# A two-layer hybrid decoder on one core: the first head's gates made alone, every fourth early sum on VectorE, and identity products ahead of two TensorE stages

## The reference, cut to what matters

```python
for l in range(2):                                  # x is (1, 512, 1024) float32
    h = rmsnorm(x, norm1_g[l]); z = h @ w_in[l]     # 3080 columns
    mixed = [norm(attention(8 heads of 64)), norm(chunked_gmlp), norm(short_conv)]
    x = x + mixed @ w_out[l]
    h2 = rmsnorm(x, norm2_g[l])
    q = h2 @ w_query[l]                             # 8 heads, two halves of 128
    s1, s2 = q_half . sub_keys                      # 128 keys each
    v1, i1 = top_k(s1, 16); v2, i2 = top_k(s2, 16)
    sc, ci = top_k(v1[:, None] + v2[None, :], 16)   # 16 of 256 pairs
    expert = i1[ci // 16] * 128 + i2[ci % 16]       # one of 16384 rows
    gate = softmax(sc)
    x = x + sum_k gelu(expert_u[expert_k] . h2) * gate_k * expert_v[expert_k]
out = rmsnorm(x, final_g)
```

## The time and the profile before

| | |
|---|---|
| median of 3 executions | 2962.34 us (2959.41 to 2963.81) |
| the profiled execution | 2957.96 us, its span 2956.2 us |
| mean granted TensorE clock | 0.83 of full |
| busy: PE, DVE, ACT, POOL | 2379.9, 1981.1, 1259.0, 1236.9 us |
| DMA | 1192.27 MB, mean 403 GB/s; the gathers 1073.81 MB |

### The profile page before, as it was taken

One profiled execution on the slowest core, in us unless ns is written; L12 is line 12 of the kernel. 1 busy time (PEld: TensorE's weight loads), 2 busy tenths in 40 slices (PEclk: granted clock), 3 DMA queues, 4 the chain that ended last, 5 costly groups with the idle time before them and its releaser, 6 DMA issues.

```text
span 2956.2 us, 38032 instructions
## 1 busy us (share of the span) xinstructions
PE 2379.9 (81%) x12592; PEld 940.0 (32%) x12592; DVE 1981.1 (67%) x4731; ACT 1259.0 (43%) x3735; POOL 1236.9 (42%) x1063
## 2 busy tenths in 40 slices
PE   8799988888967887787976898888896667767665
PEld 6633445344612332242421233323351111111110
DVE  2666566887468757877448766887647777777544
ACT  2242543863344337734334434753333333333333
POOL 0232343444344434444334444444434544555452
PEclk9899988998967998897976998888897665566666
DMA  9699999999999999999999999999999999999997
GB/s 360 231 379 357 381 390 416 421 420 419 414 417 418 412 416 414 412 408 420 417 414 411 415 410 420 410 407 419 420 419 421 410 421 421 421 406 421 421 421 299
DMA packets 202349, 1192.27 MB, mean 403 GB/s; under 512 B 25384, under 2 KB 38184, under 8 KB 68520
## 3 DMA queue, kind: packets, MB, share of 16 engines
q0 software_dynamic: 147456, 1073.81, 88.2%
q1 hardware_dynamic: 54696, 116.03, 10.4%
HBM read 1187.67 MB, written 2.10 MB: 402 GB/s over the span
## 4 chain that ended last, share of the span: by engine, by line
DMA 44%; PE 32%; DVE 10%; ACT 7%; issue 6%; POOL 2%; POOLq 0%; DVEq 0%; ACTq 0%
DMA arena<-in_uv,eidx 41%; PE acc L1793 12%; PE bank L1485 9%; DVE arena L1471 5%; PE bank L1727 4%; PE bank L1567 3%; DMA unit<-in_w_in 2%; POOL arena L803 2%; ACT L1039 1%; ACT diag L1048 1%; ACT wts L1042 1%; PE heads L1485 1%; DMA unit<-in_w_query 1%; PE bank L1690 1%; ACT L936 1%
## 5 line engine op out<-in xcount | busy, mean ns | idle before, releaser
L803 POOL DMA_INDIRECT arena<-in_uv,eidx x1024 | 1202.2, 1174 | 1531.6 <-PE acc L1793 1305.4
L1793 PE MATMUL acc<-arena,diag 64*64 64x512 f32 x8192 | 1404.4, 772 | 519.1 <-ACT diag L1048 486.5
L1471 DVE CUSTOM_DVE_ANT_0 arena<-arena,h 128x1024 f32<-128x1024 f32 x1024 | 1254.2, 1226 | 771.6 <-DMA arena<-in_uv,eidx 765.0
L1039 ACT ACTIVATE gelu<-dots 128x1 f32<-128x1 f32 x1024 | 206.1, 201 | 1346.4 <-DVE dots L1471 1345.0
L1793 PEld LDWEIGHTS acc<-arena,diag 64*64 64x64 f32 x8192 | 256.6, 155 | 1357.3 <-ACT diag L1048 1170.5
L1048 ACT ACTIVATE diag<-identc,wts 128x64 f32<-128x64 f32 x1024 | 356.1, 348 | 33.6
L1042 ACT ACTIVATE wts<-gelu,gate 128x1 f32<-128x1 f32 x1024 | 301.4, 294 | 33.2
L1727 PE MATMUL bank<-h,unit 128*128 128x256 f32 (+1 forms) x1024 | 231.1, 372 | 6.9 <-DMA unit<-in_w_query 6.9
L1727 PEld LDWEIGHTS bank<-h,unit 128*128 128x128 f32 x1024 | 171.3, 195 | 116.6 <-issue 92.5
L1485 PE MATMUL bank<-unit,h 128*128 128x512 f32 (+1 forms) x336 | 139.9, 545 | 0.0
L1567 PE MATMUL bank<-h,unit 128*128 128x256 f32 (+2 forms) x480 | 125.6, 405 | 0.0
(11 more groups left out here) (207 smaller groups left out, 1735.5 us busy)
## 6 DMA issues: line engine op xcount, KB each, us to landing
unit<-in_w_in SPq DMA_DIRECT2D x36, 1024.0 KB, 20.8
unit<-in_w_query SPq DMA_DIRECT2D x35, 1024.0 KB, 12.0
arena<-in_uv,eidx POOLq DMA_INDIRECT x1024, 17.3
unit<-in_w_out SPq DMA_DIRECT2D x16, 1024.0 KB, 9.6
arena<-in_w_in SPq DMA_DIRECT2D x8, 1024.0 KB, 11.7
arena<-in_w_query SPq DMA_DIRECT2D x5, 1024.0 KB, 19.6
arena<-in_w_out SPq DMA_DIRECT2D x4, 1024.0 KB, 14.3
x<-in_x SPq DMA_DIRECT2D x4, 512.0 KB, 10.1
```

Source lines behind the costliest of these rows:

```text
L803: nc.gpsimd.indirect_dma_start(arena[:, n % NBUF, :], None, uv, bass.IndirectOffsetOnAxis(ap=eidx[:, seq % 2, j:j + 1], axis=0)).then_inc( ...
L1039: nc.scalar.activation(gelu[:, group], dots[:, group], ACT.Gelu_apprx_tanh).then_inc(s_ge, GROUP)
L1471: V.tensor_tensor_reduce(out=uu, in0=uu, in1=h_nat[seq % 3], scale=1.0, scalar=0.0, op0=ALU.mult, op1=ALU.add, accum_out=dots[:, n % BODY: ...
L1793: ins = nc.tensor.matmul(acc[rows][cols * HALF:(cols + 1) * HALF, :], diag[own, n % NBUF, :], arena[own, n % NBUF, D + f * 512:D + (f + 1) ...
```

## The change

Four parts, all in the first 128 slots or before them.

1. **Gates of the first head alone.** Ahead of slot 0 VectorE makes head 0's numbers and, at once, head 0's gates; head 1 becomes chunk 0 of the routing plan, 19 parts from slot 0 on, two a slot, its exponential at slot 5. Chunk 1 moves from slot 3, two a slot, to slot 10, three a slot. The exponential of chunk 0 is split in two, each over one head.
2. **Sums by VectorE.** Slots 11, 15, 19, ... 111 (26 of them) get no `diag` and no matmuls. VectorE adds weight times `expert_v` to `x` with one `scalar_tensor_tensor` of 128x1024, issued behind the dot two slots later. A semaphore of its own, `s_vsum`, frees these buffers.
3. **Identity products.** 12 float32 products of the 128x128 identity at TensorE's start, and 14 between the output product and `T2` of the first pass. Nothing reads their result.
4. ScalarE squares two constants into a scratch tile before it waits for `x`.

```diff
+WARM_START, WARM_NORM = 12, 14
+VEC_LAG = 2
+SECOND_HEAD, SECOND_CHUNK = (0, 2), (10, 3)
+    def on_vector(n):
+        return n % 4 == 3 and 8 <= n < SLOTS - 16
     def route_at(r):
+        if r <= 1:
+            return SECOND_HEAD if r == 0 else SECOND_CHUNK
-        return (3, 2) if r == 1 else (first_slot(p) + 27 * (c - 1) + ..., 1)
# GpSimd, ScalarE: buffer n - NBUF
-                    pool.wait_ge(s_used, n - NBUF + 1)
+                    wait_summed(pool, n - NBUF)      # s_vsum if on_vector, else s_used
# ScalarE
             act.wait_ge(s_setup, 10)
+            nc.scalar.activation(junk16[:, 0:2], ones[:], ACT.Square)
...
+                if on_vector(n):
+                    continue                          # no diag
# VectorE, first pass
                 if p == 0:
-                    for _ in routing(l, 0, 0):
-                        pass
+                    first_head(l, 0)
+                    ask_exp(0, 1)
+                    take_gates(0, 0, 0, 1, 0)
+            def add_weighted(n):
+                t = tile_of[n // SLOTS]
+                dve.wait_ge(s_wt, n + 1)
+                if sums_by_vector(n):
+                    dve.wait_ge(s_vsum, sums_by_vector(n))
+                V.scalar_tensor_tensor(out=x[:, t, :], in0=arena[:, n % NBUF, D:2 * D], scalar=wts[:, n % BODY:n % BODY + 1],
+                                       in1=x[:, t, :], op0=ALU.mult, op1=ALU.add).then_inc(s_vsum, 1)
...                                                   # in the slot loop, behind the dot of slot n
+                if n >= VEC_LAG and on_vector(n - VEC_LAG):
+                    add_weighted(n - VEC_LAG)
# TensorE
+                if p == 0:
+                    wait_freed(pe, p, "CS")
+                    keep_clock(WARM_NORM)
                 yield from idle(NORM_STEPS)           # then T2
+            def keep_clock(n):
+                for _ in range(n):
+                    mm(acc[1][:, 0:P], ident[:], ident[:], True, True)
             pe.wait_ge(s_setup, 10)
+            keep_clock(WARM_START)
...                                                   # in the slot loop
+                if on_vector(n):
+                    continue                          # no matmuls
+                pe.wait_ge(s_dg, sums_by_tensor(n + 1))
```

More of the change, by code:

```diff
@@ L335, in due, with sums_by_tensor, sums_by_vector @@
         return steps_done(n) if n >= 0 else steps_ahead()
+    def on_vector(n):
+        return n % 4 == 3 and 8 <= n < SLOTS - 16
+    def sums_by_tensor(n):
+        return sum(not on_vector(m) for m in range(n))
+    def sums_by_vector(n):
+        return sum(on_vector(m) for m in range(n))
     def route_at(r):
         seq = r // CHUNKS
+        if r <= 1:
+            return SECOND_HEAD if r == 0 else SECOND_CHUNK
         if seq in first_seq and r % CHUNKS == 0:
@@ L343, in route_at, with route_parts, gates_no @@
         c = r - first_seq[p] * CHUNKS
-        return (3, 2) if r == 1 else (first_slot(p) + 27 * (c - 1) + (5 if p == 0 else 0), 1)
+        return first_slot(p) + 27 * (c - 1) + (5 if p == 0 else 0), 1
+    def route_parts(r):
+        return 26 if r else 19
     def routes(n):
-        return [r for r in range(1, NSLOTS // CS) if 0 <= n - route_at(r)[0] < -(-26 // route_at(r)[1])]
+        return [r for r in range(NSLOTS // CS) if 0 <= n - route_at(r)[0] < -(-route_parts(r) // route_at(r)[1])]
     def exp_slot(r):
         a, n = route_at(r)
-        return a + 15 // n + 1
+        return a + (15 if r else 8) // n + 1
+    def gates_no(r):
+        return r + 1
     def chunk_no(seq, c):
@@ L543, in trunk_kernel @@
         s_dg = sem("diag_ready")
-        s_used = sem("slots_free")
+        s_used = sem("slots_summed_by_tensor")
+        s_vsum = sem("slots_summed_by_vector")
         s_xe = sem("x_with_experts")
@@ L569, in wait_freed, with wait_summed @@
             eng.wait_ge(free[k], n + 1)
+        def wait_summed(eng, n):
+            if on_vector(n):
+                eng.wait_ge(s_vsum, sums_by_vector(n + 1))
+            else:
+                eng.wait_ge(s_used, sums_by_tensor(n + 1))
         def unit_no(p, *key):
@@ L836, in square, with gate_exp @@
                 nc.scalar.activation(out[:, 0:src.shape[1]], src, ACT.Square, accum_out=total).then_inc(s_sq, 1)
-            def gate_exp(seq, c):
-                act.wait_ge(s_gexp, chunk_no(seq, c) + 1)
-                nc.scalar.activation(top, top, ACT.Exp).then_inc(s_sc, 1)
+            def gate_exp(nth, lo, hi):
+                act.wait_ge(s_gexp, nth + 1)
+                nc.scalar.activation(top[:, lo:hi, :], top[:, lo:hi, :], ACT.Exp).then_inc(s_sc, 1)
             roots = [0]
@@ L1007, in dense @@
                         if (c, e) == (4, TAKE_AT + 1):
-                            gate_exp(0, 0)
+                            gate_exp(0, 0, 1)
                         yield 1
@@ L1033, in _ @@
                         if exp_slot(r) == n + g:
-                            gate_exp(r // CHUNKS, r % CHUNKS)
-                if j % CS == 0:
-                    act.wait_ge(s_gates, chunk_no(seq, j // CS) + 1)
+                            gate_exp(gates_no(r), 0 if r else 1, HC)
+                if n == 0:
+                    act.wait_ge(s_gates, 1)
+                elif n == K:
+                    act.wait_ge(s_gates, gates_no(0) + 1)
+                elif j % CS == 0:
+                    act.wait_ge(s_gates, gates_no(chunk_no(seq, j // CS)) + 1)
                 group = slice(b, b + GROUP)
@@ L1043, in _ @@
                                          scale=gate[:, seq % 2, j + g:j + g + 1]).then_inc(s_wt, 1)
+                if on_vector(n):
+                    continue
                 act.wait_ge(s_wt, n + GROUP)
-                if n + GROUP > NBUF:
-                    act.wait_ge(s_used, n + GROUP - NBUF)
+                if n >= NBUF:
+                    wait_summed(act, n - NBUF)
                 for g in range(GROUP):
@@ L1073, in ask_roots, with ask_exp, take_gates @@
                 roots[0] += 1
-            def routing(l, seq, c):
[L1076 to L1084, removed]
-                yield 1
[L1086 to L1091, removed]
+            def ask_exp(lo, hi):
+                step(V.tensor_copy(dn[:, lo:hi], top[:, lo:hi, 0]))
+                V.tensor_tensor(top[:, lo:hi, :], top[:, lo:hi, :], dn[:, lo:hi].unsqueeze(2).broadcast_to([P, hi - lo, K]),
+                                ALU.subtract).then_inc(s_gexp, 1)
+            def take_gates(seq, c, lo, hi, nth):
+                dve.wait_ge(s_sc, nth + 1)
+                step(V.tensor_reduce(dn[:, lo:hi], top[:, lo:hi, :], AX.X, ALU.add))
+                step(V.reciprocal(dn[:, lo:hi], dn[:, lo:hi]))
+                V.tensor_tensor(gate[:, seq % 2, c * CS + lo * K:c * CS + hi * K].rearrange("p (h k) -> p h k", h=hi - lo),
+                                top[:, lo:hi, :], dn[:, lo:hi].unsqueeze(2).broadcast_to([P, hi - lo, K]),
+                                ALU.mult).then_inc(s_gates, 1)
+            def routing(l, seq, c):
+                r = chunk_no(seq, c)
+                lo = 0 if r else 1
+                for k in range(lo, HC):
+                    yield from topk_head(seq, c * HC + k, k)
+                ask_exp(lo, HC)
+                yield 1
+                yield from expert_numbers(l, seq, c, lo, HC)
+                take_gates(seq, c, lo, HC, gates_no(r))
             def first_head(l, seq):
@@ L1424, in dense @@
                 if p == 0:
-                    for _ in routing(l, 0, 0):
-                        pass
+                    first_head(l, 0)
+                    ask_exp(0, 1)
+                    take_gates(0, 0, 0, 1, 0)
                 yield from idle((NQ - 2) * unit_steps(nt) + tail_steps(p))
             def add_experts(seq, t):
-                dve.wait_ge(s_used, (seq + 1) * SLOTS)
+                dve.wait_ge(s_used, sums_by_tensor((seq + 1) * SLOTS))
+                if sums_by_vector((seq + 1) * SLOTS):
+                    dve.wait_ge(s_vsum, sums_by_vector((seq + 1) * SLOTS))
                 low, high = slice(0, HALF), slice(HALF, P)
@@ L1786, in _ @@
                     pe.wait_ge(s_xe, seq)
-                pe.wait_ge(s_dg, n + 1)
+                if on_vector(n):
+                    continue
+                pe.wait_ge(s_dg, sums_by_tensor(n + 1))
                 for rows in range(2):
```

## The result

The changed kernel takes 2945.71 us (median of 5, 2942.6 to 2948.03) beside 2961.45 for the kernel before (median of 5): ratio 0.9949, 95% interval [0.9938, 0.996], so 15.7 us faster; 2942.6 was forecast, in a range of 2932 to 2956. The profiled executions are 12.1 us apart (2957.96 and 2945.85), since the one of before lies 3.5 us under its median.

The account below looks back on a forecast made before the run. The gathers' full DMA queue was taken to set the end, with TensorE bounding 162.8 to 340 us. Gains of 1.0 + 3.1 + 3 + 12.6 + 0 = 19.7 us from 2962.3 gave 2942.6, range 2932 to 2956.

Parts of the forecast that it names:

- The bound: Whole kernel: the gathers' full DMA queue sets the end, and a lead gained before 443 us is kept.
- Part 1: Ahead of the first gather: an earlier input stage and a held TensorE clock gain 1.0 + 3.1 us.
- The 1.0: Kernel's start: T1 at the full clock and without the table load in its path gains 1.0 us, bounds 2.8 to -0.4.
- The 3.1: Before T2: 14 identity products hold the clock, so query products and first gather come 3.1 us sooner.
- Part 2: First slots: the new routing order brings the first dot about 8 us sooner, worth 3 us, the queue's hole.
- It has the room: Slots 14 to 18: VectorE fits 11 parts and added sums, about 10 us, beside TensorE's 19.5 us.
- Part 3: 162.5 to 340 us, the stretch TensorE bounds: twelve sums moved to VectorE gain 12.6 us.
- rival C: From slot 31 on, VectorE takes over as the bound through waits for weights: 16 us slower, 2978; chance 0.07.
- The mixed stretch: 340 to 411 us, chain over ScalarE, TensorE and VectorE: 0 gained, bounds 4 gained, 6 lost.
- A: 162 to 340 us: DMA share 0.96 is the queue's true measure, so relief is worth half, 2954; chance 0.13.
- B: Only the first two forecast parts work, weight waits return the sums' saving: 4 us gained, 2958; chance 0.08.
- D: Before T2: identity products hold it up, 3.1 becomes -1, 2947; chance counted inside the forecast's 0.72.

Follow-up runs that it names:

- e11: As e8, but VectorE's sums end at slot 71, so ten go back to TensorE; 2941.84 us, ratio 0.9928 to the kernel before.
- e8: Changed kernel with chunk 1 at two parts a slot from slot 10 and VectorE's first sum at slot 19, not 11; 2942.68 us, ratio 0.9933.
- e2: Changed kernel without the 14 identity products ahead of T2; 2948.34 us, ratio 0.9954 to the kernel before.
- e6: Changed kernel without VectorE's sums, identity products and early square, so the new routing alone; 2967.86 us, ratio 1.0017 to the kernel before.
- e14: The routing alone again, e6 unedited, in different rounds; 2962.6 us, ratio 1.0007 to the kernel before.
- e15: The kernel before again, unedited, a single run with a second trace; 2962.09 us.
- e4: Changed kernel with chunk 1 at two parts a slot (slots 10 to 22) in place of three; 2940.89 us, ratio 0.9932.
- e12: Changed kernel with e4's chunk 1 and VectorE's sums from slot 11, every third slot in 20 to 75, else every fourth; 2935.56 us, ratio 0.9916.
- e3: Changed kernel with the routing of the kernel before, both heads of chunk 0 ahead of slot 0; 2947.7 us, ratio 0.9953.
- e1: Changed kernel with no sums by VectorE; 2958.29 us, ratio 0.9989 to the kernel before.
- e10: As e8, but every third slot in 20 to 75 is VectorE's in place of every fourth; 2940.12 us, ratio 0.9921.
- e13: The changed kernel again, unedited; 2945.48 us, ratio 0.9952 to the kernel before.

## Why the prediction was right, and where it was not

**The bound** was read rightly. The lead that the changed kernel has at gather 105 (11.8 us) is still there at the last gather (12.8), and the spans differ by 12.1. In between it is 16.1 at gather 110 and 14.4 at gather 200, so it is kept within some 4 us and not to the tenth, and a good agreement at one gather is chance. The sentence that nothing in the change touches the work behind 443 us was not exact: three of the added sums start at 444, 462 and 477 us. e11, which leaves them out, is no slower than e8, which has them.

Of the signs named, most came: the first dot starts 9.8 us behind the first gather (108.75 us), each window of 10 us from 110 to 160 has 411 to 418 GB/s, and from 380 to 443 us the queue moves 413 GB/s and more. The stretch moves 379 GB/s, not 390, because of the hole at its start.

**Part 1, forecast 1.0 + 3.1.** Measured 1.04 for T1's end of the chain (the first input product at 13.74 for 14.78 us), and 4.0 at the first gather. The 1.0 was right by luck. T1 began when the identity products let it, at 7.97 us, and was done 2.2 us sooner, of the 2.8 of the bounds; 1.2 of these were lost where VectorE waits until 10.5 us for a transfer, which the prediction did not count. No run leaves out the 12 products or the early square alone, so what each gives is not shown. The 3.1 was right in its mechanism and nearly in size: 7.43 us of query products became 4.48. The rule on short idle times that the prediction takes from the Trainium skill did not bite: the granted clock was 1.00 from 88 to 92 us, in the query products, in all nine traces with the 14 products, and 0.50 to 0.64 in the five without them (before, e2, e6, e14, e15). The argument that T1 ran at the lower level although the column shows full was right too: behind the identity products it takes 1.95 us.

**Part 2, forecast 3 gained: wrong in size, measured as nothing within the noise.** The step that failed is "It has the room", said of VectorE at slots 14 to 18. It set chunk 1's 11 last parts and the sums against the 19.5 us that TensorE needs for four slots, on the mean. But VectorE was the chain up to the dot of slot 14 already in the kernel before (its row at 160.60 us above), and there it needs the parts, the five `h` instructions and the sum of slot 11 in one row. The lead at gather 9 was real (13.7 us) but did not last: it filled the nine buffers sooner, while TensorE's sum of slot 14 came only 2.5 us sooner, 1.5 less than part 1 had given. TensorE, idle for 7 of the 10 us before, then began the stretch at the lower clock (so did e4; the kernel before did not). The lost time appears 9 slots later as the queue's hole at 170 to 190 us. e4 and e12, which have another density of chunk 1, reach the sum of slot 14 in 57.0 us from the first gather and not 61.3, and the queue's hole is less than half as deep in e4: it was the density. As it stands the new order gains 1 us by e3 and costs 2 by e14, neither told apart from nothing, and e1's and e14's 60.1 us lie between the two traces of the kernel before (59.8 and 62.5).

**Part 3, forecast 12.6.** e1 puts it at 12 (with the few sums outside the stretch in it); the stretch is 13.2 us shorter with 12 sums less. In the table it is 13.7 from gather 30 to 75. The bounds from rows 3 and 4 held: VectorE at 112.9 of 164.3 us never became the chain in the stretch, which is TensorE's from 162.3 us on. Its waits for weights, 7.1 us in five of 26, are the wait that rival C needed, and too small. GpSimd waited for an added sum ten times, 40 us in all, in a time in which it waits for TensorE otherwise.

**The mixed stretch, forecast 0.** The table shows a loss of 4 from gather 75 to 90 in the changed kernel. e3 and e4 show the same, and e1 loses 3.4 with no sums at all, while e12 loses 0.4 and e14 nothing. At gather 110 it is back in the changed kernel but for 0.5. What is left lies inside the bounds taken (6 lost); the cause of the swing was not isolated.

**The rivals.** A (the share 0.96 is the measure of the queue) falls: in e12 the same stretch moves 407 GB/s at a share of 1.01, so 363 at 0.96 did have room. B falls with e1, C with the measured time (16 slower was its price). D did not come: T2 starts 1.1 us earlier. The total is 4 us short of the forecast's 19.7, which is about what part 2 failed to bring. The sum of terms with what was measured: 4.0 + 12 - 1 for the rest is 15, and the time says 15.7.

## What to carry to other kernels

When a transfer queue is the final bound, follow the issue time of its n-th transfer against the other kernel's: a part that is kept shows as a step that stays, and a lead that melts within the buffers' depth was only a fuller buffer. Two traces of one kernel say how large a step must be to mean anything (2.7 us here). A shorter head start on an in-order engine is worth only what its next dense place lets through, so spread what was moved behind before counting it; here one number, three parts a slot or two, was worth about 5 us beside the 16. Moving a quarter of one engine's sums to one with room paid 12 us in the stretch where the first is the chain, and nothing that could be measured beside it (e11).

## What the runs showed of the hardware that was not expected

The TensorE clock between 65 and 70 us, where nothing differs between the programs that share part 1, came out either way: at 1.00 from 67 to 70 us in e1, e2, e3, e4, e8 and e11, and at 0.50 to 0.68 in the changed kernel, e10, e12 and e13. The changed kernel and e1, window 67 to 70:

```profile
67.00:70.00 3.00, 3.00 (x11) 2.48 (x10) 1.43 (x3) 0.00 (x0) 1.33 (x1) 0.68 1.05 382
```

```profile
67.00:70.00 3.00, 3.00 (x15) 2.64 (x14) 2.11 (x5) 0.00 (x0) 1.25 (x1) 1.00 1.06 388
```

With the clock kept, the first gather is 5.8 us ahead and not 4.0. In e10 the clock had fallen once before, to 0.50 from 14 to 16 us behind 2.6 us in which TensorE was idle, and its first gather is only 2.4 us ahead. A difference of 2 us between two profiles is therefore no evidence for an edit here, and the two traces of the kernel before differ by 4.0 us at gather 30 (e15). The first gathers also met, in one set of four runs, the 7 us gap of ScalarE (6.8 to 7.4): the engines' streams stood still there with no semaphore of the program behind it that the profile shows. Its cause is not known.

Switching ScalarE's table cost 1.28 us, as the earlier trace rows has it, with the next instruction 0.02 us behind; the Trainium skill, "ScalarE: Activation LUTs", section "What ACT_TABLE_LOAD costs", states about 2.66 us with a drain. In the changed kernel's slot 5 two switches and an exponential took 2.8 us, from 125.19 to 128.01, so the measurement decides for the shorter one here.
